# Where a gated delta-rule layer adds its cumulative gates, and when ScalarE splits the next weights

## The reference

```
proj = hn @ w_in
qkv  = silu(causal_depthwise_conv_2(proj[..., :3 * DN_DIM], conv_w))   # 4 taps
z    = proj[..., 3 * DN_DIM:4 * DN_DIM]
g    = -exp(a_log) * softplus(a_raw + dt_bias)
gc   = cumsum(g)                                    # in a chunk
decay = exp(where(tri_incl, gc[:, None] - gc[None, :], -inf))
a_low = where(tri_strict, (k_beta @ k.T) * decay, 0)
sol   = triangular_solve(a_low + eye, [v * beta, k_beta * exp(gc)])
attn_intra = (q @ k.T) * decay
```

## Time and profile before

| | |
|---|---|
| median of 3 runs | 1165.19 us |
| the profiled execution | 1166.74 us |
| its span in the trace | 1164.9 us |
| TensorE matmul busy | 1129.4 us (97%) |
| VectorE busy | 751.6 us (65%) |
| ScalarE busy | 561.3 us (48%) |
| GpSimd busy | 234.0 us (20%) |

### The profile page before, as it was taken

How to read it: one execution, slowest core, us unless ns; L and a number is a source line. 1 busy time by engine, 2 the same in 40 slices (tenths; PEclk the granted TensorE clock), 3 DMA queues, 4 the chain that set the end, 5 groups by cost and what they waited for, 6 DMA issues and landing times.

```text
span 1164.9 us, 21825 instructions
## 1 busy us (share of the span) xinstructions
PE 1129.4 (97%) x8900; PEld 1092.9 (94%) x8900; DVE 751.6 (65%) x914; ACT 561.3 (48%) x724; POOL 234.0 (20%) x230
## 2 busy tenths in 40 slices
PE   6999999999999999999999999999989999999997
PEld 6999899999999999999999888899989999888996
DVE  6647885675666544699796777753367657776333
ACT  6446557545454332655734555543344445554331
POOL 1995003302000000267844010000030002000001
PEclk9999999999999999999999999999999999999998
DMA  9664443645565455345500356555535545555541
GB/s 291 202 221 157 133 133 103 231 157 174 181 196 192 153 209 174 123 145 181 180 3 2 92 173 202 183 181 180 181 121 185 165 143 177 187 181 180 181 143 37
DMA packets 154947, 187.33 MB, mean 161 GB/s; under 512 B 6496, under 2 KB 143872, under 8 KB 154880
## 3 DMA queue, kind: packets, MB, share of 16 engines
q1 hardware_dynamic: 151312, 184.06, 48.5%
q10 hardware_dynamic: 3568, 2.31, 0.7%
HBM read 185.29 MB, written 1.07 MB: 160 GB/s over the span
## 4 chain that ended last, share of the span: by engine, by line
PE 87%; DVE 9%; ACT 1%; issue 1%; DMA 1%; SPq 0%; POOLq 0%; POOL 0%; DVEq 0%
PE PS L378 20%; PE PS L379 20%; PE PS L380 20%; PE PS L434 10%; PE PS L436 5%; DVE WL L374 2%; DVE XHL L531 1%; PE PS L1880 1%; PE PS L1866 1%; PE PS L723 1%; DVE QKV L1489 1%; PE PS L1807 1%; PE PS L673 1%; PE PS L1737 1%; DMA RAW<-in_w_in 1%
## 5 line engine op out<-in xcount | busy, mean ns | idle before, releaser
L374 DVE TENSOR_TENSOR WL<-RAW,WH 128x2048 fp32r<-128x2048 f32 x171 | 400.7, 2344 | 232.8 <-ACT WH L365 232.8
L365 ACT ACTIVATE WH<-RAW 128x2048 fp32r<-128x2048 f32 x171 | 326.5, 1910 | 225.3 <-PE PS L380 206.8
L378 PE MATMUL PS<-XHL,WH 128*128 128x256 f32 x1184 | 341.4, 288 | 13.5 <-DVE WL L327 7.4
L379 PE MATMUL PS<-XHL,WH 128*128 128x256 f32 x1184 | 336.0, 284 | 0.0
L380 PE MATMUL PS<-XHL,WL 128*128 128x256 f32 x1184 | 335.9, 284 | 0.0
L378 PEld LDWEIGHTS PS<-XHL,WH 128*128 128x128 f32 x1184 | 228.2, 193 | 18.3 <-DVE XHL L531 11.3
L379 PEld LDWEIGHTS PS<-XHL,WH 128*128 128x128 f32 x1184 | 228.4, 193 | 0.3
L380 PEld LDWEIGHTS PS<-XHL,WL 128*128 128x128 f32 x1184 | 228.1, 193 | 0.0
L378 PE MATMUL PS<-HH,WH 128*128 (+1 forms) x688 | 195.0, 283 | 4.3 <-DVE SG L1657 2.8
L380 PE MATMUL PS<-HH,WL 128*128 (+1 forms) x688 | 194.7, 283 | 0.0
L379 PE MATMUL PS<-HL,WH 128*128 (+1 forms) x688 | 194.7, 283 | 0.0
(11 more groups left out here) (291 smaller groups left out, 1554.9 us busy)
## 6 DMA issues: line engine op xcount, KB each, us to landing
RAW<-in_mlp_w_up SPq DMA_DIRECT2D x32, 1024.0 KB, 5.5
RAW<-in_mlp_w_down SPq DMA_DIRECT2D x32, 1024.0 KB, 4.9
RAW<-in_w_in SPq DMA_DIRECT2D x26, 1024.0 KB, 5.1
RAW<-in_w_ffn_in_pairs SPq DMA_DIRECT2D x22, 1024.0 KB, 5.1
RAW<-in_dn_w_in SPq DMA_DIRECT2D x16, 1024.0 KB, 5.7
RAW<-in_mb_w_in SPq DMA_DIRECT2D x12, 1024.0 KB, 5.1
RAW<-in_w_ffn_out SPq DMA_DIRECT2D x11, 1024.0 KB, 5.0
RAW<-in_w_attn_out SPq DMA_DIRECT2D x4, 1024.0 KB, 5.1
```

Of the source, the lines that this page charges most:

```text
L365: act.activation(WH[:, k], RAW[:, k], ACT.Copy).then_inc(hi_done, 1)
L374: dve.tensor_tensor(WL[:, k], RAW[:, k], WH[:, k].bitcast(F32), ALU.subtract).then_inc(lo_done, 1)
L378: pe.matmul(out, wh, xh, start=start, stop=False, skip_group_check=True)
L379: pe.matmul(out, wh, xl, start=False, stop=False, skip_group_check=True)
```

## The change

Four things move.

- The additions of GC go from GpSimd to VectorE, into `exponents`. `exponents(g)` is now called one step earlier for g = 0, 1, 2 (steps 9, 10, 11 of `dq`) and with step 0 of `dz` for g = 3.
- TensorE calls `decay_rows(2)` after step 10 of `dq` and `decay_rows(3)` after step 11, where it was 11 and step 0 of `dz`.
- GpSimd scales H right after the products with beta, ahead of CM and AMF.
- On ScalarE the waits for the readout (`freed`) and for GpSimd's tap (`tapped`) stand ahead of `split_hi` in each `dq` step, and the steps 3 to 8 become a loop.

```diff
@@ GpSimd
-            pool.wait_ge(s_.gc_done, 1)
-            for g in range(4):
-                r = slice(4 * g, 4 * g + 4)
-                by = GC[:, r, None].to_broadcast([P, 4, P])
-                pool.wait_ge(s_.b_read, g + 1)
-                pool.tensor_tensor(AM[:, r], AM[:, r], by, ALU.add).then_inc(s_.dt_ready, 1)
-                pool.tensor_tensor(AT[:, r], AT[:, r], by, ALU.subtract).then_inc(s_.dt_ready, 1)
             for g in range(4):
                 am = AM[:, 4 * g:4 * g + 4]
                 pool.wait_ge(s_.d_done, 2 * g + 1)
                 pool.tensor_tensor(am, am, BETA[:, 4 * g:4 * g + 4, None].to_broadcast([P, 4, P]), ALU.mult).then_inc(s_.ab_done, 1)
+            pool.wait_ge(s_.rh_ready, 1)
+            pool.wait_ge(s_.xl_ready, 12)
+            pool.wait_ge(s_.ba_done, 1)
+            pc(pool.tensor_tensor(H[:], H[:], RH[:, None, :].to_broadcast([P, KB, TOK]), ALU.mult))
+            pc.wait(pool)
+            pool.tensor_tensor(H[:], H[:], VEC[:, fg:fg + KB, None].to_broadcast([P, KB, TOK]), ALU.mult).then_inc(s_.h2, 1)
...
-            pool.wait_ge(s_.amf_out, STEPS)
...
@@ ScalarE
             def dq(st):
+                if st.i is not None or st.j >= 1:
+                    act.wait_ge(freed[slot_of(st, -1)], st.uses(-1))
+                if st.i is not None or st.j >= 3:
+                    act.wait_ge(s_.tapped, st.local(-3))
                 split_hi(act, st)
...
                 if st.i is not None or st.j >= 1:
-                    act.wait_ge(freed[slot_of(st, -1)], st.uses(-1))
                     tap0(st)
                 if st.i is not None or st.j >= 3:
-                    act.wait_ge(s_.tapped, st.local(-3))
                     silu(st)
-            for st in (Step(seg["dq"], j, None) for j in range(seg["dq"].n)):
-                dq(st)
+            steps(act, seg["dq"], dq, head=3, tail=3)
             for st in (Step(seg["dz"], j, None) for j in range(4)):
                 q = Step(seg["dq"], seg["dq"].n + st.j, None)
-                split_hi(act, st)
                 if st.j == 0:
                     act.wait_ge(freed[slot_of(q, -1)], q.uses(-1))
                     tap0(q)
+                split_hi(act, st)
@@ VectorE
-                if st.i is None and st.j >= 10:
-                    exponents(st.j - 10)
+                if st.i is None and st.j >= 9:
+                    exponents(st.j - 9)
...
                 dve.tensor_tensor(AT[:, r], NEGU[:, None, :].to_broadcast([P, 4, P]), four(6 + g % 2), ALU.add).then_inc(s_.b_read, 1)
+                ch.wait(dve, ch.n)
+                dve.tensor_tensor(AM[:, r], AM[:, r], per_head(GC[:, r]), ALU.add).then_inc(s_.dt_ready, 1)
+                dve.wait_ge(s_.b_read, g + 1)
+                dve.tensor_tensor(AT[:, r], AT[:, r], per_head(GC[:, r]), ALU.subtract).then_inc(s_.dt_ready, 1)
...
-                if st.j < 2:
-                    exponents(st.j + 2)
+                if st.j == 0:
+                    exponents(3)
@@ TensorE
-                if st.i is None and st.j == 11:
-                    decay_rows(2)
+                if st.i is None and st.j >= 10:
+                    decay_rows(st.j - 8)
...
-                if st.j == 0:
-                    decay_rows(3)
```

## The result

The changed kernel takes **1173.45 us** (median of 4 runs, 1173.37 to 1175.54), and the kernel before, timed beside it, 1165.85 (4 runs, 1164.81 to 1166.74). The ratio is 1.0073, with a 95% interval from 1.0056 to 1.0089: slower, by 7.6 us between the medians. I had forecast 1170.0 within 1166.0 to 1175.5. The direction and the range held; the size was too small. By the profiled executions it is 1173.36 us against 1166.74, spans 1171.6 against 1164.9: 6.7 us more. The 7.6 us lean on few runs. All 21 executions of the changed kernel have a median of 1173.66, and the kernel before, timed again beside the experiments, gave 1166.97 to 1168.30, which is 5.4 to 6.7 us less.

What follows compares the result with a forecast made beforehand. The prediction took TensorE as the bound (87% of the chain), with VectorE almost without room in dq. Terms 1.7 + 3.1 + 0 = 4.8 us on a median of 1165.19 gave 1170.0 us, range 1166.0 to 1175.5.

Steps and rivals of the forecast that it cites:

- First: the exponents one step earlier: End of dq into dz: TensorE's stall moves one step ahead, VectorE's additions cost time; 1.4 to 2.0 us, taken as 1.7.
- the mark: TensorE's first matmul of dz step 1, at 557.23 us before; forecast at about 562.
- Second: ScalarE's order and loop: dq steps on ScalarE: later splits and two table loads make VectorE late by 3.1 us, bounds 0.5 to 6.6.
- d: How much later than before VectorE ends the taps of dq step 9 (543.69 us); taken as 3.1 us.
- my courses: Two courses of VectorE's lateness through the dq steps, ending at 2.6 or 3.6 us after steps 7 and 8.
- Third: H earlier: GpSimd between the products with beta and CM: scaling H there fits in spare time; 0 us, bound 2.3.
- part one: The cost of the exponents one step earlier with additions on VectorE, at the end of dq; 1.7 us.
- Hidden: Rival: in dq, TensorE's lead absorbs ScalarE's changed order; d about 0.5, sum 1.9 us, time 1167.1 us; chance 14%.
- Not slower: Rival: the stall before decay_rows(2) goes and none comes; 1.3 us gained, time 1163.9 us; chance 5%.
- H in the way: Rival: GpSimd's H product delays VectorE's RNC reciprocals, or CM comes late; 2.5 us over forecast, 1172.5 us; chance 9%.
- GpSimd first in most steps: Rival: in most dq loop steps GpSimd precedes VectorE, or both loads count fully; sum 8.6 us, 1173.8 us; chance 14%.

Runs made afterwards that it cites:

- e1: The changed kernel with ScalarE's program as it was before: written out, split first, waits behind it; ratio 1.0024 to the kernel before.
- e3: The changed kernel with ScalarE's dq steps written out instead of looped, waits still ahead of the split; ratio 1.0025 to the kernel before.
- e12: e3 with a one-column copy on ScalarE ahead of the split in steps 3 to 8; ratio 1.0064 to the kernel before.
- e11: e3 with a one-column activation from another table ahead of the splits of steps 3 and 6, forcing table loads; ratio 1.0024 to the kernel before.
- e7: The kernel before with only GpSimd's scaling of H moved ahead of CM; ratio 0.9991 to the kernel before.
- e2: The kernel before with only ScalarE's part of the change, waits ahead of the split and the loop; ratio 1.0060 to the kernel before.
- e13: The changed kernel with a one-column product on GpSimd ahead of each add of the last tap; ratio 1.0047 to the kernel before.

## Why the prediction was right in direction and too small in size

**First: the exponents one step earlier, 1.7 us.** Right. In the changed kernel the mark comes 563.93 - 548.62 = 15.31 us after the end of the taps of step 9; before, 557.23 - 543.69 = 13.54. The difference is 1.77 us, and e1 gives 1.67. The stall moved a step ahead, as the step says. Its cause is the additions on VectorE: 0.78 and 1.53 us, GpSimd's product between the two, near the upper end of 2.4 us that I had left open. The wait of 1 to 2 us that I named before `decay_rows(3)` doesn't appear in the changed kernel. It is there in e1 (1.33); in the changed kernel TensorE went through part of step 11 at half clock and so came to it late.

**Second: ScalarE's order and loop, d = 3.1 us.** This is the step that failed, as a term that was mis-sized: d is 548.62 - 543.69 = 4.93 us. The end of the taps, step by step, against the end of the same taps before:

| at the end of the taps of | d measured | added | my courses |
|---|---|---|---|
| step 3 | 2.03 | | 1.4 or 2.1 |
| steps 4 and 5 | 2.97 | 0.94 | 1.9 or 2.9 in all |
| step 6 (second load) | 3.76 | 0.79 | + 0.4 |
| steps 7 and 8 | 4.72 | 0.96 | + 0.3 or 0.4 |
| step 9 | 4.93 | 0.21 | 0 |

(The end of the taps is the start of the next split less the idle time before it: 512.49 - 0.48 - 509.98 = 2.03.) Up to step 5 the slower of my two courses came true. After it I had GpSimd's turn as an exception that an early add makes good again. It was the rule: GpSimd goes in first in each of the steps 4, 5, 7 and 8, by 0.02 to 0.2 us, at 0.46 to 0.49 us a step. The second load cost twice what I gave it, 0.79 instead of 0.4. I had the mechanism and its place among the rivals, at 14%, and with 0.8 us a step its price was too high, as mine was too low. Taking the middle of two courses, 3.1, was also a choice against the row I had: release and split need 5.4 to 5.6 us and the step 5.62, so the register work alone decides.

By the runs the 5.00 us of lateness over e1 are: the order 1.17 (e3 over e1), a delay of about 0.1 us ahead of each split 2.37 (e12 over e3), and the changed kernel over e12 1.46, in the two steps with a load ahead of the split. The loads by themselves measured 0.92 in e11, where the first of them ran in part ahead of the wait. By these two their share is 0.92 to 1.46 us, and the larger part of the loop's price is the lost turn. That the loop's register work is that delay is inferred from 0.12 us against 0.03; a loop without loads, or with the old order, was not tried.

The Trainium skill's drain behind each load ("ScalarE: Activation LUTs", section "What ACT_TABLE_LOAD costs") would have made the sum 7.6 us, by an estimate from the page's figure (two drains, 2.8 us), so near the measured difference, and for the wrong reason: the load at 503.64 took 1.28 us and the next activation began at 504.93, so this trace shows no drain.

**Third: H earlier, 0.** Right: e7 measures 0.9991 [0.9979, 1.0004], and after the change CM still waits 2.04 us for VectorE.

**Sum.** 1.77 + 4.93 + 0 = 6.70 us, the difference of the spans. The method of adding part one and d holds. The parts measured each by itself don't add up (1.67 and 7.55 make 9.2), because the clock stretch that lies open in e2, 2.56 us, is under a wait in the changed kernel.

**Rivals.** Hidden: the order alone, without the loop, already makes VectorE 1.17 us late (e3 over e1), where that rival gave 0.5 to the whole second part. Not slower: e1, without any of that lateness, still has a wait before each of the two groups of rows. H in the way: e7. GpSimd first in most steps, 1173.8: the nearest to what happened in its mechanism. In its sum, 8.6 us, it is as far above the 6.70 of the profiles as my 4.8 is below. That its 1173.8 lies so near the median of 1173.45 is luck.

## What to carry to other kernels

Where two engines exclude each other and start within a tenth of a microsecond, look which goes first: the one that others wait for has to, and a delay of 0.1 us on a third engine can turn it in every step of a loop. In a hardware loop count the delay between the release and the work (here 0.12 us, against 0.03 written out), and look for table loads between the wait and the work. When an earlier place for a consumer moves a wait and doesn't remove it, a later place for it may remove it.

## What the runs showed of the hardware

After a wait of 3.20 us in the changed kernel and in e12, 3.06 in e2, 2.24 in e11 and 1.98 in e13 TensorE's matmuls were 0.21 us apart, at a granted clock of 0.50, for about 3 to 5 us. After 1.91 in e13, 1.81 in e3, 1.66 in the changed kernel, 1.09 before and 1.23 and 1.33 in e1 they kept their 0.12 us. So a wait can cost more than its length, and how much of it is seen depends on what TensorE would have waited for next.

Two instructions of VectorE in a row that both read two inputs from SBUF let a waiting instruction of GpSimd in between: around GpSimd's product at 550.20 (1.31 us) the second addition took 1.53 us, the first 0.78. In the last group, at 573.10 and 573.70, with GpSimd idle, both took 0.68.
